# A fourth extra chunk place for the first model's experts, with the fetch order changed to suit it

## The chip, the cores and the metric

The kernel runs on one core of a Trainium2 chip. The metric is device time in microseconds (us) of one execution. The kernel before takes 2479.06 us, the median of three runs (2478.96 to 2481.82).

## The reference, cut to what matters

Two small models run one after the other on 256 tokens of width 1024, two layers each, all in float32. Every layer has a mixer (attention in the first model; retention, an RWKV recurrence and a short convolution in the second) and then a layer of 32 experts of which every token uses two. The change lies in the expert layers of the first model:

```python
def hierarchical_moe(xn, w_group, w_router, w_gate, w_up, w_down):
    ...
    group_p = jax.nn.softmax((xt @ w_group).astype(jnp.float32), axis=-1)
    group_w, group_id = lax.top_k(group_p, 1)
    ...
    top_logits, local_id = lax.top_k(in_group, TOP_K_IN_GROUP)      # 2 of 4 experts in the group
    ...
    def expert_block(args):
        xb, e = args
        h = jax.nn.silu(xb @ w_gate[e]) * (xb @ w_up[e])            # 1024 -> 256
        return h @ w_down[e]                                        # 256 -> 1024
    ...
    y = jax.ops.segment_sum(contrib, tok_sorted, num_segments=T)
```

## The kernel before, in words

**Weights.** All weights come from HBM in chunks of 128 x 4096 float32 (2 MB), each by one DMA that SP (SyncE) issues in program order on one hardware queue. They land in `ring`, six places of that size. A chunk's arrival counts on `w_loaded`, its last use by TensorE on `w_used`; SP waits for `w_used` before it lets a new chunk overwrite a place.

**The expert layer** is the function `moe`. It is called four times: for both layers of the first model (experts 256 wide, "shared" in the code; here stage 1 and stage 2) and for both layers of the second (experts 512 wide). Experts go by quads, four at a time, eight quads in all. In the first model a quad has six chunks: 0 to 3 hold gate and up weights, 4 and 5 the down weights. I write (2,3) for chunk 3 of quad 2, and count quads from 0. A quad's work is an *item*: up to 32 tokens of each of its four experts. If an expert of the quad has more tokens, the quad is done again with the next 32, so the number of items depends on the data; every engine loops over a count that VectorE works out.

**One item on TensorE**, in its own order: gate and up products (L2031, 64 records), `combine` of the item before (L1990: the weighted sum of its outputs back to the tokens, 16 records), `gather` of the next item's tokens (L1982, 32 records), two pairs of transposes (L2042, L2046), and the down products (L2056, 32 records, half of them for chunk 4 and half for chunk 5). The first item has no item before it, so its `combine` multiplies tables that GpSimd has set to zero (L2124, L2125). The gather of item 1 waits for a one-hot table from VectorE (L2140), and that for the routing tables (`tables_ready`, L2216).

**Fetching in the first model** (L1921 to L1939). The ring alone would hold one quad. So three *extra places* in `arena` take chunks 0, 1 and 2 of the next quad, while the current one is in use. GpSimd waits until all three have landed (L2130), then copies each into the ring as soon as the last item of the current quad has used its place (L2131 to L2133). SP's order for quad q is: (q,3) straight into the ring after the last item of quad q-1 has used its fourth gate/up chunk; then (q+1,0), (q+1,1), (q+1,2) into the extra places, each after GpSimd has copied out what was there; then (q,4) and (q,5) after their places were used. Before the tables are ready SP can't know which item is a quad's last, so it waits for them ahead of that loop. After the loop it fetches the next layer's first six chunks as places come free.

**Before the stage** the six chunks of quad 0 and one extra chunk are fetched during the attention's output projection (L838); the other extra ones are issued at the stage's start (L1921).

**The second model's experts** have twelve chunks a quad. They use the same `moe`, with another fetch loop that has no copies.

## Time and profile before

| what | us |
|---|---|
| median of three runs | 2479.06 |
| the profiled execution | 2471.02 |
| its span, from first to last instruction | 2469.2 |
| TensorE busy | 2018.6 (82%) |
| VectorE, ScalarE, GpSimd busy | 634.9, 377.5, 205.5 |
| bytes read from HBM | 776.75 MB, 315 GB/s over the span |
| mean granted TensorE clock | 0.923 of full |

The page cuts the span into 40 slices of 61.7 us. Stage 1 (157 to 380 us) lies in slices 3 to 6, stage 2 (520 to 760 us) in slices 9 to 12, and the second model's expert layers in slices 20 to 26 and 34 to 40. In all of them the DMA engines are nearly always busy, at some 430 GB/s, and TensorE is partly idle. Outside them TensorE is busy and the DMA engines partly idle. In the listings of instructions "idle before <- releaser" says how long the engine stood idle before a group, and what ended the wait. Several instructions of one line in a row are merged into one line of a listing, with a count. Matmuls are counted twice (float32 takes two passes), so a line of 8 in the program shows as 16.

### The profile page before, as it was taken

The numbers are of one execution on the slowest core, as the hardware profiler recorded it, in microseconds if no ns is written. First come the engines' busy times: TensorE is split into PE (matmuls) and PEld (weight loads), VectorE is DVE, ScalarE is ACT, GpSimd is POOL, SyncE is SP. The second block draws the span as 40 slices with busy tenths as digits, with TensorE's granted clock in tenths as the row PEclk, the third lists the DMA queues.
The fourth block names the chain that finished last, engine by engine and source line by source line (L and its number), as shares of the span: only waits on it lengthen the run. The fifth ranks groups of instructions, "written<-read, shape, count | busy, mean of one in ns | idle before, by whom it ended". The sixth has DMA issues, their size and how long they took to land. (4 is left out here: it accounts for less than half of the span.)

```text
span 2469.2 us, 33765 instructions
## 1 busy us (share of the span) xinstructions
PE 2018.6 (82%) x14228; PEld 1282.1 (52%) x14229; DVE 634.9 (26%) x1483; ACT 377.5 (15%) x817; POOL 205.5 (8%) x140
## 2 busy tenths in 40 slices
PE   8997779998778999999866666599999998666665
PEld 6573336574334888888322222148888873222222
DVE  4651114531113245463100000032551121000001
ACT  2520001511002121101100000021221020000001
POOL 0213330214330000000000000000000000000000
PEclk9998889999889999999988888899999998888888
DMA  8569998449997241497999999963302389999997
GB/s 341 232 281 431 430 430 365 163 180 421 431 430 298 103 160 47 200 397 301 402 428 429 429 429 428 427 273 113 141 34 103 136 341 428 429 429 428 428 428 302
DMA packets 55842, 779.34 MB, mean 316 GB/s; under 512 B 6841, under 2 KB 7097, under 8 KB 8121
## 3 DMA queue, kind: packets, MB, share of 16 engines
q1 hardware_dynamic: 55736, 777.82, 75.7%
q8 instruction: 80, 1.31, 0.2%
q14 instruction: 26, 0.20, 0.0%
HBM read 776.75 MB, written 1.05 MB: 315 GB/s over the span
## 5 line engine op out<-in xcount | busy, mean ns | idle before, releaser
L2031 PE MATMUL bank<-ring,xnT 128*32 128x512 f32 x3136 | 446.8, 712 | 234.1 <-DMA ring<-in_w_exp 233.8
L2031 PEld LDWEIGHTS bank<-ring,xnT 128*32 128x32 f32 x3136 | 101.4, 121 | 573.4 <-issue 292.3
L2056 PE MATMUL bank<-ring,arena 128*32 128x512 f32 x1440 | 201.2, 696 | 148.1 <-DMA ring<-in_w_exp 126.7
L1023 PE MATMUL bank<-xnT,ring 128*128 128x256 f32 x960 | 210.7, 379 | 0.0
L1023 PEld LDWEIGHTS bank<-xnT,ring 128*128 128x128 f32 x960 | 181.6, 190 | 28.4 <-issue 4.5
L2056 PEld LDWEIGHTS bank<-ring,arena 128*32 128x32 f32 x1440 | 48.8, 120 | 273.4 <-issue 155.4
L2229 DVE TENSOR_TENSOR arena<-bank,arena 128x256 f32<-128x256 f32 (+1 forms) x33 | 18.3, 554 | 609.5 <-PE bank L2031 520.5
L1709 PE MATMUL bank<-xnT,ring 128*128 128x256 f32 x768 | 173.6, 379 | 0.0
L2133 POOL COPY ring<-arena 128x4096 f32<-128x4096 f32 x42 | 150.5, 3620 | 261.4 <-DMA arena<-in_w_exp 232.7
L1709 PEld LDWEIGHTS bank<-xnT,ring 128*128 128x128 f32 x768 | 146.1, 190 | 22.1 <-issue 2.5
L1990 PE MATMUL bank<-arena,xnT 128*128 128x256 f32 x592 | 142.0, 394 | 0.0
L1990 PEld LDWEIGHTS bank<-arena,xnT 128*128 128x128 f32 x592 | 112.7, 196 | 53.8 <-issue 35.1
L1982 PE MATMUL bank<-arena 128*128 128x128 f32 x1056 | 123.7, 275 | 0.2 <-DVE arena L2140 0.2
L1982 PEld LDWEIGHTS bank<-arena 128*128 128x128 f32 x1056 | 122.7, 192 | 2.3 <-DVE arena L2140 0.6
L251 DVE SCALAR_TENSOR_TENSOR arena<-arena 128x1024 f32<-128x1024 f32 x96 | 112.6, 1223 | 29.9 <-DMA arena<-in_w_ada 29.4
L2240 DVE COPY xnT<-bank 128x512 f32<-128x512 f32 x33 | 22.8, 692 | 320.3 <-PE bank L2056 320.3
L1716 PE MATMUL bank<-arena,ring 128*128 128x256 f32 x384 | 90.7, 379 | 0.0
L1017 PE MATMUL bank<-ring,xnT 128*128 128x512 f32 x192 | 84.4, 602 | 6.4 <-ACT xnT L375 6.4
L1716 PEld LDWEIGHTS bank<-arena,ring 128*128 128x128 f32 x384 | 73.0, 190 | 9.9
L2104 ACT ACTIVATE arena<-bank 128x256 f32<-128x256 f32 (+1 forms) x33 | 16.1, 487 | 398.7 <-PE bank L2031 398.7
L2085 ACT ACTIVATE xnT<-bank,mod,gains 128x128 f32<-128x128 f32 x64 | 24.1, 456 | 325.8 <-PE bank L1982 325.8
L1198 POOL TENSOR_TENSOR arena<-arena,pc 128x1024 f32<-128x1024 f32 x2 | 3.9, 1952 | 792.8 <-DVE arena L1300 792.8
(439 smaller groups left out, 2081.9 us busy)
## 6 DMA issues: line engine op xcount, KB each, us to landing
ring<-in_w_exp SPq DMA_DIRECT2D x238, 2048.0 KB, 25.6
arena<-in_w_exp SPq DMA_DIRECT2D x50, 2048.0 KB, 16.9
arena<-in_w_ada SPq DMA_DIRECT2D x24, 2048.0 KB, 11.3
ring<-in_w_in SPq DMA_DIRECT2D x20, 2048.0 KB, 23.2
ring<-in_w_merge SPq DMA_DIRECT2D x18, 2048.0 KB, 8.0
ring<-in_w_o SPq DMA_DIRECT2D x8, 2048.0 KB, 11.8
ring<-in_w_conv SPq DMA_DIRECT2D x6, 2048.0 KB, 8.0
ring<-in_w_rest SPq DMA_DIRECT2D x2, 1696.0 KB, 14.1
```

The source lines that it names most:

```text
L251: last = nc.vector.scalar_tensor_tensor(w, w, 1.0, c, ALU.mult, ALU.mult, accum_out=mod_sums[:, l, 4 * ch + j:4 * ch + j + 1])
L1017: last = nc.tensor.matmul(o[:, 0:MW], xnT[:, k, P * (not first):P * (not first) + P], w[:, k, :], start=k == 0, stop=k == KT - 1)
L1023: last = nc.tensor.matmul(o[:, T * j:T * j + T], w[:, k, col:col + P], xnT[:, k, :], start=k == 0, stop=k == KT - 1)
L1709: last = nc.tensor.matmul(bank[m % 8][:, 0:T], w[:, k, P * (d % 4):P * (d % 4) + P], xnT[:, k, :], start=k == 0, stop=k == KT - 1)
L1716: last = nc.tensor.matmul(bank[m % 8][:, T:2 * T], w[:, k, P * d:P * d + P], ys[i][:, k, :], start=k == 0, stop=k == MT - 1)
L1982: last = nc.tensor.matmul(gather_banks[d // 4][:, P * (d % 4):P * (d % 4) + P], xtok[:, t, P * d:P * d + P], onehot[:, t, :], start=t == 0 ...
L1990: last = nc.tensor.matmul(bank[d // 2][:, T * (d % 2):T * (d % 2) + T], Yw[:, P * d:P * d + P], gwT, start=False, stop=ready is not None, ...
L2031: last = nc.tensor.matmul(o[rows(e), :], Xw[:, k, rows(e)], w[:, at:at + MW], start=k == 0, stop=k == KT - 1)
L2056: last = nc.tensor.matmul(o[rows(e), :], hidT[:, j, rows(e)], w[:, at:at + MW], start=j == 0, stop=j == ft - 1)
L2085: last = nc.scalar.activation(Xw[:, d, :], at_d, ACT.Identity, scale=gain[:, d:d + 1], bias=shift[:, d:d + 1])
L2133: nc.gpsimd.tensor_copy(ring[:, place(r0 + n), :], extra[spots[n]]).then_inc(w_loaded(slot(n)), 16)
L2240: nc.vector.tensor_copy(Yw[:, 0:MW], y0_bank[:, :]).then_inc(y0_taken, 1)
```

## The change

- `EXTRA1` goes from 3 to 4: all four gate/up chunks of the next quad have an extra place. GpSimd copies four chunks a quad in place of three, and waits for four landings first.
- SP's order for quad q becomes (q,4), then (q+1,0) to (q+1,3), then (q,5). The first fetch of a quad now waits for the last item's first *down* chunk (`w_used`, `n0 + EXTRA1 + 1`).
- The extra places become consecutive. The third one covers ground in `arena` where the stage's small tables and the vector `c_all` lay. The tables move to `small`. `c_all` moves to the part of the constants that only the second model uses. That part (1032 of 2429 columns) is therefore not loaded at the start; it is loaded in stage 2, behind the next layer's vectors, and the first model's final norm waits for it.
- The first item of every expert layer, in both models, no longer runs `combine`. GpSimd no longer sets those two tables to zero.

```diff
-EXTRA1, EXTRA2 = 3, 4
+EXTRA1, EXTRA2 = 4, 4
...
-        c_all = ar(15744, D)
+        CST2 = CONST["ret_in"][0]
+        c_all = cst[:, CST2:CST2 + D]
...
-                    sp.dma_start(cst[:], dram["consts"]).then_inc(cst_loaded, 16)
+                    sp.dma_start(cst[:, 0:CST2], dram["consts"][:, 0:CST2]).then_inc(cst_loaded, 16)
...
-            at = 13824
+            at = 0 if shared else SMALL2
             extras = EXTRA1 if shared else EXTRA2
-            spots = (0, 1, 3) if shared else (0, 1, 2, 3)
...
                     if after:
                         vectors_early(sp, *after, 1 - turn[0])
+                    if shared and after[0] == 2:
+                        sp.dma_start(cst[:, CST2:], dram["consts"][:, CST2:]).then_inc(cst2_loaded, 16)
...
                             for n in range(EXTRA1 if q + 1 < NQ else 0):
                                 sp.wait_ge(w_loaded(slot(n)), 16 * ((r0 + n) // RING + 1) + 16 * q)
-                                sp.dma_start(extra[spots[n]], feed(q + 1, n)).then_inc(extra_in, 16)
+                                sp.dma_start(extra[n], feed(q + 1, n)).then_inc(extra_in, 16)
...
                         pe.wait_ge(y0_taken, it + 1)
-                        pe.wait_ge(gwT_ready, it + 1)
-                        combine()
+                        if not first_item:
+                            pe.wait_ge(gwT_ready, it + 1)
+                            combine()
...
-                    nc.gpsimd.memset(gate_tab[:, NE * TT:(NQ + 1) * QUAD * TT], 0.0)
-                    nc.gpsimd.memset(gwT, 0.0)
-                    nc.gpsimd.memset(Yw, 0.0).then_inc(gwT_ready, 1)
+                    nc.gpsimd.memset(gate_tab[:, NE * TT:(NQ + 1) * QUAD * TT], 0.0).then_inc(gwT_ready, 1)
...
                         dve.wait_ge(gw_turned, it + 1)
+                        dve.wait_ge(gwT_ready, it + 1)
                         nc.vector.tensor_copy(gwT, y0_bank[:, 0:T]).then_inc(gwT_ready, 1)
```

SP's queue at the start of stage 1, before. L1921 fills the extra places, L225 loads the next layer's vectors, L1916 is a fetch into the ring and L1936 one into an extra place:

```order
L1921 DMA arena<-in_w_exp1 128x4096 x2
L225 DMA vec<-in_vec1 128x27 [waits e1_tables]
L225 DMA row<-in_row1 1x8
L225 DMA small<-in_small1 128x2880
L1931 TENSOR_LOAD offs
L1931 ISA x2
L1932 REGISTER_ALU
L1916 DMA ring<-in_w_exp1 128x4096 [waits w_used0]
L1936 DMA arena<-in_w_exp1 128x4096 [waits w_loaded0_0]
L1936 DMA arena<-in_w_exp1 128x4096 [waits w_loaded0_1]
L1936 DMA arena<-in_w_exp1 128x4096 [waits w_loaded0_2]
L1938 REGISTER_ALU
```

And now (the same places have the lines L1922, L1917 and L1939):

```order
L1922 DMA arena<-in_w_exp1 128x4096 x3
L225 DMA vec<-in_vec1 128x27 [waits e1_tables]
L225 DMA row<-in_row1 1x8
L225 DMA small<-in_small1 128x2880
L1934 TENSOR_LOAD offs
L1934 ISA x2
L1935 REGISTER_ALU
L1917 DMA ring<-in_w_exp1 128x4096 [waits w_used0]
L1939 DMA arena<-in_w_exp1 128x4096 [waits w_loaded0_0]
L1939 DMA arena<-in_w_exp1 128x4096 [waits w_loaded0_1]
L1939 DMA arena<-in_w_exp1 128x4096 [waits w_loaded0_2]
L1939 DMA arena<-in_w_exp1 128x4096 [waits w_loaded0_3]
```

Three chunks stand ahead of the tables in place of two. The ring fetch behind them was (1,3) and is now (1,4), and its wait on `w_used` is for one chunk more of the item. Everything behind it in the queue stands behind that wait.

TensorE in the first item of stage 1, before, from its last gate/up chunk to the transposes:

```order
L2031 MATMUL bank<-ring,xnT 32x512 [waits w_loaded0_3]
L2031 MATMUL bank<-ring,xnT 32x512 x7
L1990 MATMUL bank<-arena,xnT 128x256 [waits e1_gwT,e1_y0taken]
L1990 MATMUL bank<-arena,xnT 128x256 x7
L1982 MATMUL bank<-arena 128x128 [waits e1_onehot]
L1982 MATMUL bank<-arena 128x128 x15
L2042 MATMUL bank<-cst,arena 128x128 [waits e1_hid]
L2042 MATMUL bank<-cst,arena 128x128
```

And now:

```order
L2034 MATMUL bank<-ring,xnT 32x512 [waits w_loaded0_3]
L2034 MATMUL bank<-ring,xnT 32x512 x7
L1985 MATMUL bank<-arena 128x128 [waits e1_onehot,e1_y0taken]
L1985 MATMUL bank<-arena 128x128 x15
L2046 MATMUL bank<-cst,arena 128x128 [waits e1_hid]
L2046 MATMUL bank<-cst,arena 128x128
```

The eight matmuls of `combine` are gone, and the gather's wait for the one-hot table stands right behind the gate/up products.

## Rows read from the trace of the kernel before

**Rows 1.** The page: DMA share by slice, and the costliest groups of the expert stages.

```profile
DMA  8569998449997241497999999963302389999997
...
L2031 PE MATMUL bank<-ring,xnT 128*32 128x512 f32 x3136 | 446.8, 712 | 234.1 <-DMA ring<-in_w_exp 233.8
...
L2133 POOL COPY ring<-arena 128x4096 f32<-128x4096 f32 x42 | 150.5, 3620 | 261.4 <-DMA arena<-in_w_exp 232.7
```

**Rows 2.** Stage 2, stretches: PE, PEld, DVE, ACT, POOL busy; clock, DMA share, GB/s.

```profile
530.00:540.00 10.00, 10.00 (x80) 5.46 (x73) 4.85 (x27) 0.38 (x1) 0.00 (x0) 1.00 0.70 275
540.00:550.00 10.00, 8.79 (x83) 4.86 (x85) 2.91 (x8) 2.10 (x6) 0.00 (x0) 1.00 0.00 0
550.00:560.00 10.00, 10.00 (x80) 5.81 (x73) 0.42 (x1) 0.38 (x1) 9.71 (x3) 1.00 0.39 129
```

**Rows 3.** TensorE in stage 1, in time: start, length, what, idle before.

```profile
177.27 3.84 PE L1982 MATMUL bank<-arena 128*128 128x128 f32 x32 [0.16 <-DVE arena L2140]
...
182.70 3.64 PE L2056 MATMUL bank<-ring,arena 128*32 128x512 f32 x32 [1.16 <-ACT arena L2109]
...
205.11 3.51 PE L2056 MATMUL bank<-ring,arena 128*32 128x512 f32 x16 [4.02 <-DMA ring<-in_w_exp]
...
351.16 3.64 PE L2056 MATMUL bank<-ring,arena 128*32 128x512 f32 x16 [7.72 <-DMA ring<-in_w_exp]
355.96 1.92 PE L2056 MATMUL bank<-ring,arena 128*32 128x512 f32 x16 [1.16 <-DMA ring<-in_w_exp]
357.92 7.07 PE L2031 MATMUL bank<-ring,xnT 128*32 128x512 f32 x64
364.93 3.72 PE L1990 MATMUL bank<-arena,xnT 128*128 128x256 f32 x16
...
369.61 3.64 PE L2056 MATMUL bank<-ring,arena 128*32 128x512 f32 x32 [0.53 <-DVE arena L2234]
```

**Rows 4.** TensorE in stage 2, in time.

```profile
539.18 3.73 PE L1982 MATMUL bank<-arena 128*128 128x128 f32 x32
...
544.51 3.64 PE L2056 MATMUL bank<-ring,arena 128*32 128x512 f32 x32 [1.16 <-ACT arena L2109]
...
564.09 3.64 PE L2056 MATMUL bank<-ring,arena 128*32 128x512 f32 x32 [1.16 <-ACT arena L2109]
...
733.75 3.64 PE L2056 MATMUL bank<-ring,arena 128*32 128x512 f32 x16 [1.16 <-DMA ring<-in_w_exp]
```

**Rows 5.** VectorE in time: the one-hot table, in stage 1 and 2.

```profile
174.37 2.84 DVE L2140 TENSOR_TENSOR arena<-cst,arena 128x256 f32<-128x256 f32 x1 [2.07 <-issue]
...
536.31 0.43 DVE L2140 TENSOR_TENSOR arena<-cst,arena 128x256 f32<-128x256 f32 x1 [1.78 <-issue]
```

**Rows 6.** SP in time: the first ring fetch of stage 1 and 2.

```profile
174.31 0.33 SPq L1916 DMA_DIRECT2D ring<-in_w_exp  x1
...
555.33 0.33 SPq L1916 DMA_DIRECT2D ring<-in_w_exp  x1
```

**Rows 7.** One microsecond stretches in stage 1, columns as in group 2.

```profile
171.00:172.00 1.00, 1.00 (x14) 0.27 (x10) 0.97 (x12) 0.00 (x0) 0.00 (x0) 1.00 0.24 98
172.00:173.00 1.00, 1.00 (x16) 0.25 (x8) 0.23 (x3) 0.00 (x0) 0.00 (x0) 1.00 0.00 0
```

**Rows 8.** GpSimd in time: first and last group of copies in stage 1.

```profile
173.34 10.88 POOL L2133 COPY ring<-arena 128x4096 f32<-128x4096 f32 x3 [15.00 <-DMA arena<-in_w_exp]
...
346.33 10.69 POOL L2133 COPY ring<-arena 128x4096 f32<-128x4096 f32 x3 [18.52 <-DMA arena<-in_w_exp]
```

**Rows 9.** VectorE in time, at the program's start.

```profile
9.53 0.17 DVE L296 CAST arena<-arena 128x4 f32<-128x4 int32 x1 [9.40 <-DMA arena<-in_positions]
...
17.73 3.26 DVE L367 SCALAR_TENSOR_TENSOR xnT<-hT,vec,arena 128x256 f32<-128x256 f32 x8 [0.31 <-PEq L278]
```

**Rows 10.** TensorE in the second model's first expert layer, in time.

```profile
1196.56 4.71 PE L1990 MATMUL bank<-arena,xnT 128*128 128x256 f32 x16
...
1223.99 1.92 PE L2031 MATMUL bank<-ring,xnT 128*32 128x512 f32 x16 [1.43 <-DMA ring<-in_w_exp]
```

More of the change, by code:

```diff
@@ L75, in constants @@
         put(f"freq{half}", np.tile(freq.astype(np.float32)[None, :], (P, 1)))
+    put("pair", p[:, None] % HD == np.arange(HEADS // 2)[None, :])
+    put("iota", np.tile(np.arange(1.0, 33.0)[None, :], (P, 1)))
     lg = np.log1p(-np.exp2(-5.0 - np.arange(RH, dtype=np.float32))).astype(np.float32)
@@ L87, in constants @@
     put("unit", at == to)
-    put("pair", p[:, None] % HD == np.arange(HEADS // 2)[None, :])
-    put("iota", np.tile(np.arange(1.0, 33.0)[None, :], (P, 1)))
     put("inner", np.tile((np.arange(T) % CH != 0)[None, :], (P, 1)))
@@ L259, in build @@
         c_loaded = sem("c_loaded")
+        cst2_loaded = sem("cst2_loaded")
         def sines(act, c_ready):
@@ L1878, in ar @@
                 size = int(np.prod(shape))
-                v = (arena[0:n, o:o + size] if shared else small[0:n, o - at + SMALL2:o - at + SMALL2 + size])
+                v = small[0:n, o:o + size]
                 if len(shape) == 2:
@@ L1920, in _ @@
                             continue
-                        sp.dma_start(extra[spots[e]], feed(1, e) if shared else feed(0, kept + e)).then_inc(extra_in, 16)
+                        sp.dma_start(extra[e], feed(1, e) if shared else feed(0, kept + e)).then_inc(extra_in, 16)
                     for n in range(RING, kept):
@@ L2010, in here @@
                                 pe.wait_ge(extra_in, 16 * extras)
-                                return extra[spots[n - kept]]
+                                return extra[n - kept]
                             if first_item and held:
@@ L2132, in _ @@
                                 pool.wait_ge(w_used(), last_item + (n0 + n + 1))
-                                nc.gpsimd.tensor_copy(ring[:, place(r0 + n), :], extra[spots[n]]).then_inc(w_loaded(slot(n)), 16)
+                                nc.gpsimd.tensor_copy(ring[:, place(r0 + n), :], extra[n]).then_inc(w_loaded(slot(n)), 16)
                 @block.vector
@@ L2280, in _ @@
                     norm_sums(pe, norms, bank[0])
+                    pe.wait_ge(cst2_loaded, 16)
                 @block.vector
@@ L2310, in build @@
                 head_rms_out(l, ada, extra_in)
-                moe("e1", lambda q, n: dram["w_exp1"][l, 6 * q + n], MOE1, F1, extra_in, (2,), NG1, gains[:, 1, :], None, None, (1, 1) if l + 1 < L else (2, 0))
+                moe("e1", lambda q, n: dram["w_exp1"][l, 6 * q + n], MOE1, F1, extra_in, (3,), NG1, gains[:, 1, :], None, None, (1, 1) if l + 1 < L else (2, 0))
                 next_layer(MOE1)
```

## The prediction

> **What bounds the kernel now.** I read the page first. The line of DMA shares shows 9 in the slices of the expert stages, and TensorE's costliest group, the gate/up products, stands idle 234.1 us of which 233.8 us end with a weight's landing [rows 1]. So in these stages the transfers decide, not the matmuls. Then I read stage 1 in order of time: the down products of quad 1 wait until 205.11 us for chunk 4, those of quad 6 until 351.16 us [rows 3]. Between them lie five quads of six chunks, so a chunk takes (351.16 - 205.11) / 30 = 4.868 us, and a quad 29.2 us. TensorE needs less: one item is 19.6 us where nothing waits (544.51 to 564.09 us) [rows 4]. Third, I looked for stretches without transfers inside the stages, because only there can another place help. In stage 1 the hole is short, about 2.5 us near 172 us [rows 7]. In stage 2 it is long: the DMA share is 0.70, 0.00 and 0.39 in three stretches of 10 us [rows 2]. There quad 0 has two items, and SP may not fetch (1,3) before the second has used its gate/up chunks, at 555.33 us [rows 6].
>
> **What ends a stage.** This decides the sum, so it comes before the parts. The last landing that TensorE waits for in stage 1 is (6,5): its products start at 355.96 us. From there on nothing waits for a transfer: item 7 runs 357.92, 364.93, 369.61 us, and the wait before the last is 0.53 us for VectorE [rows 3]. So the stage's end is the landing of (6,5) plus a fixed chain on TensorE. Now count the chunks that the queue carries from the first ring fetch through (6,5). Before: (1,3), (1,4), (1,5), the 30 chunks of quads 2 to 6, and (7,0) to (7,2), which is 36. After: (1,4), (1,5), the same 30, and (7,0) to (7,3), which is 36 again. The fourth place takes (1,3) out at the front and puts (7,3) in at the back. Nothing is saved on the way. What matters is when the queue starts again, and how long the chain behind (6,5) is.
>
> **The later restart.** Seen from TensorE, the stream of 36 chunks began at 355.96 - 36 x 4.868 = 180.7 us in stage 1 and at 733.75 - 175.2 = 558.5 us in stage 2 [rows 3, 4]. In stage 2 the queue was empty when (1,3) was issued, so issue to effective start costs 558.5 - 555.33 = 3.2 us [rows 6].
> - Stage 2 after. (1,4) waits for the first down chunk of item 1. Its products began at 564.09 us and half of them are done 1.8 us later, at 565.9 us [rows 4]. The removed `combine` of item 0 gives some of it back, but not its whole 3.7 us: the gather that then follows needs the one-hot table, which ends at 536.31 + 0.43 = 536.74 us, while the gather now starts at 539.18 us [rows 4, 5]. So 2.4 us. (1,4) is issued at about 563.6 us, the stream starts at 566.8 us: +8.3 us.
> - Stage 1 after. The same with one item: half the down products at 182.70 + 1.8 = 184.5 us [rows 3]. The gather can start when the table is there. It took 2.84 us beside GpSimd's copies, which began at 173.34 us, against 0.43 us in stage 2 where GpSimd waits [rows 5, 8]. After, GpSimd waits for a fourth landing, some 4.9 us later, so I take 0.43 us: table at 174.8 us, gather 2.4 us earlier than its 177.27 us. (1,4) is issued at 182.2 us and the stream starts at 185.4 us: +4.7 us. By then the queue is empty: one chunk more ends at about 171.3 + 4.9 = 176.2 us, and the next layer's small table (1.5 MB, 3.4 us at the rate of a chunk) near 180 us. If the one-hot table took 2.84 us after all, it would be +7.1 us.
>
> The Trainium skill, "DMA: Bandwidth & Descriptors", in its part on the chain of events of a DMA, gives a fixed cost of about 2.0 us beside the bytes. The 3.2 us that I read are more than that; with 2.0 us both restarts would be 1.2 us earlier and the sum below 2.4 us smaller. I stay with the row.
>
> **The longer chain behind (6,5).** GpSimd began its last three copies 9.6 us before (6,5) was there and took 10.7 us [rows 8]. In the new order (7,3) is the last before (6,5), so the copies begin one chunk time, about 4.8 us, before it, and there are four: 4 x 3.6 = 14.4 us [rows 1]. The last ends 9.6 us after the landing and its products 1.8 us later: 11.4 us. Before, the gate/up products ended at 364.99 us, 9.0 us after [rows 3]. Each stage: +2.4 us. TensorE now gets these chunks at the pace of the copies, half of the time busy. After 7.72 us of waiting 16 records took 3.64 us, the lower clock level of 1.2 GHz, and the next 16 after 1.16 us of waiting 1.92 us, at 2.4 GHz [rows 3]. If the last gate/up chunk and the `combine` behind it run low, they cost 1.8 and 1.0 us more (4.71 us against 3.72 us for a `combine` behind such a stretch) [rows 3, 10]. Bounds 0 and 2.8 us a stage, also if all is at the high level; I take 0.5 us each, since copies at 3.6 us leave shorter waits than those before 351.16 us.
>
> The Trainium skill speaks against the change here: "TensorE: Matmul & The Clock Gate", section "HAM oscillation — how this bites in real kernels", says that bursts of matmuls shorter than the transfer wait between them all start on the slow clock. By that rule the sum would be 4.6 us higher (2 x 2.8 instead of 2 x 0.5). The trace agrees at 351.16 us and not at 355.96 us.
>
> **The start.** 1032 of 2429 columns of the constants, 0.53 MB, leave the queue ahead of the positions. VectorE waits for these until 9.53 us and its chain then runs to the norm at 17.73 us [rows 9]. At 430 GB/s that is 1.2 us earlier, and everything behind it: -1.2 us (bounds -1.2 and 0, if TensorE's or ScalarE's chain is next).
>
> **Edits that I cost at nothing.** The other half of the constants, 1.2 us of transfer, falls into the hole of stage 2 [rows 2]; without the hole it would be +1.2 us. 14 more copies (50.7 us) fit into GpSimd's waits, 18.5 us a quad [rows 8]. The zeroed tables were off the path. In the second model the first `combine` (4.71 us) goes too, but the queue behind is never empty and TensorE soon waits for a chunk again, at 1223.99 us [rows 10]: 0, at best -0.5 us. VectorE's new wait is for the copy of the item before, long done. The moved tables are read by the same instructions.
>
> **The sum**, against the profiled execution of 2471.0 us: -1.2 + (4.7 + 2.4 + 0.5) + (8.3 + 2.4 + 0.5) = +17.6 us, so 2488.6 us. Behind each stage TensorE has no wait for a weight until the mixer, so the delay is passed on. The three timed runs had a median 8.0 us above the profiled one; carried over, 2496.7 us. I say 2496 us.
>
> **The rivals.**
> - *A hole in every quad* (10%). (q+1,4) waits for the first down chunk of quad q, and all extra chunks stand behind it. The copies for quad q end 19.6 us before the landing of (q,5), gate/up 17.8 us; from there to the down products it is 8.8 us (555.3 to 564.09 us) [rows 4, 6], and 1.8 us for half of them: issue 7.2 us before, seen 8.1 us later at the earliest, which is 4.0 us earlier than the stream needs it. If slow clocks and slower tables take 5 us instead of the 2.8 us above, 1 us is lost in each of five quads of both stages: +10 us, 2507 us. For it speaks the 3.64 us row, against it that the margin is 4 us.
> - *The last landing sets the end* (8%). If (7,5) and the next layer's chunks behind it decided, each stage would get its chunk back: -1.2 + (4.7 - 4.9) + (8.3 - 4.9) = +2.0 us, 2481 us. Against it stand the 0.53 us wait and the missing DMA waits behind 355.96 us [rows 3].
> - *The other side: one chunk less in the bound stretch* (6%). If, besides, the restart were not later, because the queue lasts until the first down chunk is used, the time would be -1.2 - 2 x 4.9 = -11 us, 2468 us. It decides whether the queue is still full at 182 and at 564 us. For stage 1 only 2 us are missing; in stage 2 the queue is empty more than 20 us before.
> - The forecast has 74%, its own range 2490 to 2502 us; 2% is for what I don't see.
>
> **How the numbers follow.** What this measurement can tell from no change is about 0.2%, 5 us. Slower: 74 + 10 + 2 = 86%. Same: 7%. Faster: 7%. The range of 2483 to 2508 us holds the forecast with the bounds of its terms and the lower part of the holes; it leaves out the last two rivals, 14%.
>
> **What would show it.** In the trace after: the first ring fetch of the stages at about 181 and 561 us (182.2 and 563.6 us less the 1.2 us of the start, the second plus the 7.6 us of stage 1, so near 570 us); DMA share 1.00 from there until item 7; the last quad's gate/up products in four bursts 3.6 us apart; the norm behind stage 1 at some 6.4 us later than now. It is wrong if TensorE waits for (7,5), if the first ring fetch is issued while the queue is still busy, or if a stretch inside quads 2 to 6 shows a DMA share well below 1.

## The result, and the profile after

The changed kernel takes 2497.64 us, the median of seven runs (2487.99 to 2504.74). The kernel before, run beside it on the same chip, took 2479.06 us (seven runs, 2473.29 to 2481.82). The ratio is 1.0078, with a 95% interval of 1.006 to 1.0096: slower by 0.8%. The forecast was 2496 us.

The profiled execution after took 2499.79 us with a span of 2497.9 us and a mean granted clock of 0.916, against 2471.02, 2469.2 and 0.923 before. The page after, as in [rows 1] (DMA share by slice, then line, engine, operation, count | busy us, mean ns of one | idle before, and what ended it):

```profile
DMA  8569998448997331397899999963312379999997
...
L2034 PE MATMUL bank<-ring,xnT 128*32 128x512 f32 x3136 | 460.2, 727 | 247.3 <-DMA ring<-in_w_exp 236.5
...
L2135 POOL COPY ring<-arena 128x4096 f32<-128x4096 f32 x56 | 201.5, 3641 | 246.0 <-DMA arena<-in_w_exp 215.4
```

The DMA line hardly shows the change: of the slices of stages 1 and 2 only the tenth (562 to 624 us of the span after) goes from 9 to 8, since the hole of stage 2 now reaches into it. The gate/up products wait 13.2 us longer in all, and only 2.7 us more of it for DMA. The other waits go from 0.3 to 10.8 us, 10.5 us of them for GpSimd's copies. These are now 56 and not 42, at the same length.

The page shows where, the rows in time show how much. The same stretches of stage 2 after (columns as in [rows 2]):

```profile
560.00:570.00 10.00, 8.84 (x64) 7.46 (x68) 2.68 (x7) 1.90 (x6) 9.20 (x3) 1.00 0.00 0
570.00:580.00 10.00, 9.98 (x91) 3.19 (x84) 1.12 (x2) 0.97 (x2) 0.00 (x0) 1.00 0.82 323
```

In stage 1 the hole is short, but it is there before the restart too:

```profile
178.00:180.00 2.00, 1.38 (x16) 0.59 (x20) 1.82 (x3) 0.00 (x0) 2.00 (x1) 1.00 0.08 33
```

SP after, the first ring fetch of stages 1 and 2 and the fetches behind it (as in [rows 6]):

```profile
180.59 0.33 SPq L1917 DMA_DIRECT2D ring<-in_w_exp  x1
180.97 3.21 SPq L1939 DMA_DIRECT2D arena<-in_w_exp  x2
...
570.75 0.33 SPq L1917 DMA_DIRECT2D ring<-in_w_exp  x1
571.12 2.41 SPq L1939 DMA_DIRECT2D arena<-in_w_exp  x4
```

The prediction had these at about 181 and near 570 us. TensorE at the start of stage 1 after (start, length, what, idle before and what ended it; compare the first two rows of [rows 3]):

```profile
173.21 3.81 PE L1985 MATMUL bank<-arena 128*128 128x128 f32 x32 [1.50 <-DVE arena L2142]
...
178.62 3.64 PE L2060 MATMUL bank<-ring,arena 128*32 128x512 f32 x32 [1.16 <-ACT arena L2113]
```

178.62 us and half of 3.64 us is 180.44 us; the fetch is issued at 180.59 us. So it does wait for the first half of the down products. And TensorE at the end of stage 1 after, the last five rows of [rows 3]:

```profile
350.68 1.92 PE L2060 MATMUL bank<-ring,arena 128*32 128x512 f32 x16 [1.16 <-ACT arena L2113]
359.38 3.64 PE L2060 MATMUL bank<-ring,arena 128*32 128x512 f32 x16 [6.78 <-DMA ring<-in_w_exp]
362.80 5.89 PE L2034 MATMUL bank<-ring,xnT 128*32 128x512 f32 x48
368.95 1.92 PE L2034 MATMUL bank<-ring,xnT 128*32 128x512 f32 x16 [0.26 <-POOL ring L2135]
370.81 3.72 PE L1993 MATMUL bank<-arena,xnT 128*128 128x256 f32 x16
375.48 3.64 PE L2060 MATMUL bank<-ring,arena 128*32 128x512 f32 x32 [0.52 <-DVE arena L2237]
```

The landing of (6,5) is the last one waited for, at 359.38 us; there is no DMA wait behind it, so (7,5) doesn't set the end. The last gate/up chunk waits for GpSimd and is done at 370.87 us, 11.5 us after the landing; 11.4 us was the sum. GpSimd after, the last quad but one and the last (as in [rows 8]):

```profile
325.46 14.42 POOL L2135 COPY ring<-arena 128x4096 f32<-128x4096 f32 x4 [14.72 <-DMA arena<-in_w_exp]
354.67 14.23 POOL L2135 COPY ring<-arena 128x4096 f32<-128x4096 f32 x4 [14.78 <-DMA arena<-in_w_exp]
```

**The ledger.** I take as a stage's start its first transposes of the tokens (L1964 before, L1967 after) and as its end the first matmul of the norm behind it (L361, L363). All in us, from the two profiled executions:

| part of the program | before | after | difference |
|---|---|---|---|
| start to stage 1 | 157.14 | 155.39 | -1.75 |
| stage 1, to the landing of (6,5) | 198.82 | 203.99 | +5.17 |
| stage 1, landing to the end | 20.78 | 23.23 | +2.45 |
| between the stages | 143.69 | 141.70 | -1.99 |
| stage 2, to the landing of (6,5) | 213.32 | 224.60 | +11.28 |
| stage 2, landing to the end | 22.50 | 23.19 | +0.69 |
| behind stage 2 | 1712.95 | 1725.80 | +12.85 |
| span | 2469.2 | 2497.9 | +28.7 |

The start and the two stages make +17.8 us, close to the difference of the medians (18.6 us). The two other rows need not be the change. Behind stage 2 the first experiment below speaks for that: it has the program of before there, word for word, and takes 1726.2 us (2498.3 - 772.08).

### The profile page after: what moved, and what is told of

Its sections match the earlier page's. It is cut to its first block and busy times, and to the rows that moved or that the text cites. A ratio compares the mean times of both kernels' runs of the same rounds, so it can differ in the third digit from the quotient of the medians.

```text
span 2497.9 us, 33692 instructions
## 1 busy us (share of the span) xinstructions
PE 2022.7 (81%) x14164; PEld 1283.6 (51%) x14165; DVE 639.7 (26%) x1483; ACT 378.0 (15%) x817; POOL 252.0 (10%) x146
## 5 line engine op out<-in xcount | busy, mean ns | idle before, releaser
L2034 PE MATMUL bank<-ring,xnT 128*32 128x512 f32 x3136 | 460.2, 727 | 247.3 <-DMA ring<-in_w_exp 236.5
L2060 PE MATMUL bank<-ring,arena 128*32 128x512 f32 x1440 | 192.9, 672 | 159.5 <-DMA ring<-in_w_exp 125.3
L2135 POOL COPY ring<-arena 128x4096 f32<-128x4096 f32 x56 | 201.5, 3641 | 246.0 <-DMA arena<-in_w_exp 215.4
L1985 PEld LDWEIGHTS bank<-arena 128*128 128x128 f32 x1056 | 128.3, 199 | 9.5 <-issue 7.7
L1985 PE MATMUL bank<-arena 128*128 128x128 f32 x1056 | 129.8, 283 | 3.0 <-DVE arena L2142 3.0
L1993 PE MATMUL bank<-arena,xnT 128*128 128x256 f32 x528 | 126.4, 393 | 0.0
L1993 PEld LDWEIGHTS bank<-arena,xnT 128*128 128x128 f32 x528 | 100.3, 195 | 49.5 <-issue 31.6
L2115 ACT COPY xnT<-bank 128x512 f32<-128x512 f32 x33 | 19.3, 585 | 320.8 <-PE bank L2060 320.8
## 6 DMA issues: line engine op xcount, KB each, us to landing
ring<-in_w_exp SPq DMA_DIRECT2D x224, 2048.0 KB, 25.6
ring<-in_w_rest SPq DMA_DIRECT2D x2, 1696.0 KB, 10.8
```

The costliest lines, as they stand in the source:

```text
L1985: last = nc.tensor.matmul(gather_banks[d // 4][:, P * (d % 4):P * (d % 4) + P], xtok[:, t, P * d:P * d + P], onehot[:, t, :], start=t == 0 ...
L1993: last = nc.tensor.matmul(bank[d // 2][:, T * (d % 2):T * (d % 2) + T], Yw[:, P * d:P * d + P], gwT, start=False, stop=ready is not None, ...
L2034: last = nc.tensor.matmul(o[rows(e), :], Xw[:, k, rows(e)], w[:, at:at + MW], start=k == 0, stop=k == KT - 1)
L2060: last = nc.tensor.matmul(o[rows(e), :], hidT[:, j, rows(e)], w[:, at:at + MW], start=j == 0, stop=j == ft - 1)
L2115: nc.scalar.copy(Yw[:, MW:D], y1_bank[:, :]).then_inc(y1_taken, 1)
L2135: nc.gpsimd.tensor_copy(ring[:, place(r0 + n), :], extra[n]).then_inc(w_loaded(slot(n)), 16)
```

## The experiments

One table for all, from each one's profiled execution. "Fetch" is the first fetch behind the tables, (6,5) its landing, both counted from the stage's start, as is the length. The ratio is against runs of the kernel before, taken beside it on the same chip; e1 to e4 ran on one chip, e5 to e8 on another.

| kernel | ratio (95%) | stage 1: fetch, (6,5), length | stage 2: fetch, (6,5), length |
|---|---|---|---|
| before | | 17.17, 198.82, 219.60 | 34.90, 213.32, 235.82 |
| after | 1.0078 (1.006 to 1.0096) | 25.20, 203.99, 227.22 | 46.44, 224.60, 247.79 |
| e1 late restart | 1.0091 (1.0066 to 1.0116) | 27.62, 206.53, 227.29 | 46.68, 225.20, 247.48 |
| e2 zeros back | 1.012 (1.0082 to 1.0158) | 26.05, 204.71, 228.00 | 48.66, 226.85, 250.04 |
| e3 small edits alone | 1.0003 (0.9978 to 1.0028) | 17.16, 199.20, 219.96 | 34.26, 212.66, 235.21 |
| e4 extras first | 1.0025 (1.0005 to 1.0045) | 24.80, 203.50, 225.69 | 34.25, 212.41, 233.17 |
| e5 split places | 0.9959 (0.9943 to 0.9974) | 18.40, 194.64, 216.94 | 32.84, 206.11, 228.74 |
| e6 three places first | 1.0048 (1.0027 to 1.0068) | 19.83, -, 225.39 | 34.58, -, 239.03 |
| e7 one more copy | one run, 2525.86 us | 25.06, 209.14, 239.11 | 46.26, 229.74, 259.60 |
| e8 two more copies | one run, 2553.53 us | 25.21, 219.80, 253.31 | 46.19, 240.16, 273.43 |

**e1, late restart: the kernel before, and only the first ring fetch of the stage waits for the first down chunk.**

```diff
-                            sp.wait_ge(w_used(), last_item + (n0 + EXTRA1 + 1))
+                            sp.wait_ge(w_used(), last_item + (n0 + EXTRA1 + (2 if q == 1 else 1)))
                             fetch(q, EXTRA1)
```

> The kernel before with three extra places; only the first ring fetch of each stage of the first model waits, as in the changed kernel, for the first down chunk of quad 0's last item, not for its fourth gate/up chunk. No fourth place. My theory (the stage ends at the landing of (6,5) plus a fixed chain, so a later restart of the queue is paid in full): first ring fetch near 184.6 us in stage 1 (174.3 before) and 565.9 us plus the delay of stage 1 in stage 2 (555.3 before); the down products of (6,5) 7 us later in stage 1 (184.6 + 3.2 against 180.7 effective) and 10.5 us later in stage 2; no change of the chain behind (364.99 - 355.96 = 9.0 us to the end of gate/up). Sum +17.5 us, ratio 1.007. Rival 'the last landing sets the end, or other slack hides it': the norm behind each stage moves by under 2 us, ratio 1.000 to 1.002.

Measured: 2496.15 against 2473.18 us; the expected 1.007 is inside the interval. SP and TensorE of e1, first fetch of stages 1 and 2, and the last landing of stage 1:

```profile
183.23 0.33 SPq L1916 DMA_DIRECT2D ring<-in_w_exp  x1
...
571.28 0.33 SPq L1916 DMA_DIRECT2D ring<-in_w_exp  x1
```

```profile
362.14 1.92 PE L2056 MATMUL bank<-ring,arena 128*32 128x512 f32 x16 [1.15 <-DMA ring<-in_w_exp]
364.10 7.07 PE L2031 MATMUL bank<-ring,xnT 128*32 128x512 f32 x64
```

One number changed in a wait gives a loss as large as that of the whole change: the stages are 7.7 and 11.7 us longer. In stage 2 about 1.1 us of this is the clock: the first transposes took 3.58 us, where they took 1.94 us before. The chain behind the landing is here the old, short one (9.0 us, no wait for a copy). So the two terms are separate: e1 has the restart later by 7.7 us and no longer chain; the change has 5.2 us of restart and 2.45 us of chain. The 2.4 us between the two first fetches are in the main the `combine` that the change takes away and e1 keeps.

**e2, zeros back: the kernel after, with the first `combine` and its zeroed tables again.**

```diff
-                        if not first_item:
-                            pe.wait_ge(gwT_ready, it + 1)
-                            combine()
+                        pe.wait_ge(gwT_ready, it + 1)
+                        combine()
```

> The changed kernel with the first item's combine and the zeroed tables put back in all four expert layers. Theory: the gather of item 1 starts behind combine again, so in the first model's stages the first ring fetch comes about 2 us later than in the changed kernel (180.6 us and 570.8 us there), the landing of (6,5) with it; nothing in the second model, where the queue never runs dry: +4 to +4.5 us in all, ratio to before 1.0095. Rival 'all of combine is on the path, in all four layers': +3.7 us four times, +15 us, ratio 1.0135. Rival 'hidden': 0.

Measured: 2505.42 against 2473.18 us. The first fetch of stage 2 comes 2.2 us later than in the changed kernel, for 2.4 us in the sum, and the stage ends 2.25 us later. In stage 1 it is only 0.85 us. There this execution's first transposes ran at the higher clock (1.94 us for 3.35 us), and the gate/up products began 1.07 us earlier after the stage's start (8.18 us for 9.25 us). Without that it would be 1.9 us: less than in stage 2, because in the changed kernel the gather stands 1.50 us waiting for the one-hot table where `combine` was. The ratio is 0.0042 above that of the changed kernel, 10 us for the 4.1 us that I explain; the intervals overlap, so that isn't told apart from noise. The ratio alone doesn't exclude the rival "all of `combine`, in all four layers" (1.0135) either. The traces do: the stages show 1.9 and 2.2 us and not 3.7 us each, and behind stage 2 e2 takes 1727.5 us for 1725.8 us, not 7.4 us more. What is shown is that removing `combine` helps, and that without it the restart would come later still.

**e3, small edits alone: the kernel before, three places, its order of fetches, with the constants split and the first `combine` gone.** The diff is that of the change without `EXTRA1`, the places and the tables.

> The kernel before with only the two small edits: the constants' second half is loaded in stage 2, and the first item runs no combine. Three extra places and the old fetch order. Theory: start -1.2 to -1.8 us; stage 1: first ring fetch not moved relative to the stage's start (it waits for gate/up, which combine follows), so 0; stage 2: quad 0 has two items and the second comes 2.4 us earlier, so the first ring fetch, the landing of (6,5) and the stage's end 2.4 us earlier relative to the stage's start. Sum -4 us, ratio 0.9985. Rival 'nothing': ratio 1.000 and the same times in the trace. Rival 'all of combine counts': -1.5 - 4 x 3.7 = -16 us, ratio 0.9934.

Measured: 2471.98 against 2473.18 us, inconclusive by time: both the expected 0.9985 and no change at all lie inside the interval. In the trace stage 1 begins 1.65 us earlier, so the split of the constants does what it should. But the first fetch of stage 1 stands where it stood, 17.16 us after the start. With three places its wait is for the fourth gate/up chunk, ahead of `combine`. Stage 2 gets 0.6 us, where 2.4 us was expected. Counted from the stage's first gate/up products, the first fetch is indeed 2.3 us earlier (24.45 us for 26.71 us). But these products begin 1.6 us later after the stage's start than before (9.81 us for 8.19 us), because the gather ahead of them took 5.46 us, and 3.84 us in the kernel before:

```profile
520.27 5.46 PE L1986 MATMUL bank<-arena 128*128 128x128 f32 x32 [0.22 <-DVE arena L2143]
```

The granted clock was 0.50 from 522 to 524 us. This gather takes 5.46 or 5.47 us in all eight kernels of this study that have the small edits, and 3.84 us in the two without (before and e1). Why is not shown. VectorE and GpSimd of e3 show the other thing that I had used:

```profile
172.73 2.99 DVE L2143 TENSOR_TENSOR arena<-cst,arena 128x256 f32<-128x256 f32 x1 [2.08 <-issue]
...
171.85 10.88 POOL L2136 COPY ring<-arena 128x4096 f32<-128x4096 f32 x3 [16.29 <-PE bank L2035]
```

Beside GpSimd's copies the one-hot table takes 2.99 us. In the changed kernel, where these copies begin at 176.49 us, the same instruction runs before them:

```profile
172.64 0.43 DVE L2142 TENSOR_TENSOR arena<-cst,arena 128x256 f32<-128x256 f32 x1 [2.08 <-issue]
```

The forecast took 0.43 us for it, by that reason.

**e4, extras first: the kernel after, but SP's order for a quad is the four extra chunks, then (q,4) and (q,5).**

```diff
-                            sp.wait_ge(w_used(), last_item + (n0 + EXTRA1 + 1))
-                            fetch(q, EXTRA1)
                             for n in range(EXTRA1 if q + 1 < NQ else 0):
...
-                            for n in range(EXTRA1 + 1, RING):
+                            for n in range(EXTRA1, RING):
```

> The changed kernel with SP's order turned: in each quad first the four extra fetches, then (q,4), then (q,5). Theory: the queue restarts when GpSimd has copied the first chunk out (started 176.5 us in stage 1, 555.0 us in stage 2 of the changed kernel, plus 3.6 us), so first fetch behind the tables at 180.1 and 558.6 us against 180.6 and 570.8 us: -0.5 and -12 us. The copies begin two chunk times before (6,5) instead of one, so the chain behind it is bound by TensorE's 7 us of gate/up: -0.9 us a stage. Sum -14 us against the changed kernel, ratio to before 1.002. Rival 'the later restart isn't what costs; the copies or the slow clock are': the time stays within 4 us of the changed kernel, ratio 1.006 to 1.009.

Measured: 2480.68 against 2473.18 us, in the profile 2479.29 us. The restart no longer waits for the down chunk, and the first fetch of stage 2 is back at 34.25 us. SP of e4:

```profile
177.79 4.07 SPq L1937 DMA_DIRECT2D arena<-in_w_exp  x2
...
554.62 3.87 SPq L1937 DMA_DIRECT2D arena<-in_w_exp  x2
```

The ratio of 1.0025 is what was expected. Stage 2 is then 2.65 us shorter than before, where the changed kernel's was 12 us longer: the order, not the fourth place, costs stage 2. Nor does the place gain anything there: e3 has three places, e4 has four, both carry 36 chunks from a first fetch at 34.26 and 34.25 us, and (6,5) lands at 212.66 and 212.41 us. Stage 1 is still 6.1 us longer. There the first fetch waits for GpSimd's first copy, and GpSimd waits until all four extra chunks have landed.

**e5, split places: e4 with one semaphore for each extra place, and the fourth extra chunk behind (q,5).**

```diff
-                            for n in range(EXTRA1 if q + 1 < NQ else 0):
+                            for n in range(EXTRA1 - 1 if q + 1 < NQ else 0):
...
-                            for n in range(EXTRA1 + 1, RING):
+                            for n in range(EXTRA1, RING):
                                 sp.wait_ge(w_used(), last_item + (n0 + n + 1))
                                 fetch(q, n)
+                            if q + 1 < NQ:
+                                take_extra(EXTRA1 - 1)
...
-                            pool.wait_ge(extra_in, 16 * extras * q)
                             for n in range(EXTRA1):
+                                pool.wait_ge(extra_in[n], 16 * q)
```

(`take_extra(n)` is the old wait and fetch, counting on `extra_in[n]`.)

> The changed kernel with a semaphore for each extra place, so that GpSimd copies a chunk as soon as it has landed and its ring place is free, and with SP's order per quad (q+1,0), (q+1,1), (q+1,2), (q,4), (q,5), (q+1,3): no fetch waits for a down chunk before the queue has restarted, and (7,3) comes behind (6,5). Theory: through (6,5) there are now 35 chunks behind the restart, not 36, with one more fetched before it. Stage 1 seen from its start: the queue hardly runs dry, (6,5) some 3.5 us earlier than in the kernel before (198.8 us after the stage's start there), the chain behind it 10.3 us to the end of gate/up instead of 9.0: -2 us. Stage 2: restart at the first copy, -3.8 us, and one chunk less, -4.9 us, so (6,5) 8.7 us earlier (213.3 us after the stage's start before): -8 us. With the start's -1.5 us: -12 us against the kernel before, ratio 0.995. Rival 'the copies by GpSimd are the burden of the fourth place': slower than before still, 1.003 or more. Rival 'the restart decides alone, the count of chunks doesn't': -1.5 - 3.8 = -5 us, ratio 0.998.

Measured: 2464.26 us (11 runs) against 2475.3 us (18 runs): faster than the kernel before by 0.4%, and than the changed one by 1.2% (0.9959 / 1.0078). SP, GpSimd and TensorE of e5:

```profile
172.81 4.07 SPq L1937 DMA_DIRECT2D arena<-in_w_exp  x2
```

```profile
208.16 3.60 POOL L2137 COPY ring<-arena 128x4096 f32<-128x4096 f32 x1 [11.02 <-DMA arena<-in_w_exp]
213.01 3.60 POOL L2137 COPY ring<-arena 128x4096 f32<-128x4096 f32 x1 [1.25 <-DMA arena<-in_w_exp]
217.86 3.60 POOL L2137 COPY ring<-arena 128x4096 f32<-128x4096 f32 x1 [1.25 <-DMA arena<-in_w_exp]
```

```profile
344.25 3.64 PE L2062 MATMUL bank<-ring,arena 128*32 128x512 f32 x16 [5.66 <-DMA ring<-in_w_exp]
349.05 1.92 PE L2062 MATMUL bank<-ring,arena 128*32 128x512 f32 x16 [1.16 <-DMA ring<-in_w_exp]
351.01 5.36 PE L2036 MATMUL bank<-ring,xnT 128*32 128x512 f32 x48
357.70 1.92 PE L2036 MATMUL bank<-ring,xnT 128*32 128x512 f32 x16 [1.33 <-POOL ring L2137]
```

The copies follow the landings one by one. The first fetch is early again in both stages. In stage 1 that is the work of the semaphores alone, since the fourth chunk's new position changes nothing ahead of it: the copies begin 14.8 us after the stage's start, for 21.2 us in e4. And (7,3) now stands behind (6,5), so up to this landing the queue carries 35 chunks, not 36: here the fourth place does save a chunk. The landing comes 4.2 and 7.2 us earlier than in the kernel before. Counting as the prediction did for stage 2: 32.84 + 3.2 + 35 x 4.868 = 206.4 us, measured 206.11 us. In stage 1 the same count gives 192.0 us for a measured 194.64 us; there the queue wasn't empty when the first fetch was issued (DMA share 0.99 from 171 to 173 us), so the stream doesn't start at the fetch. The two edits of e5 weren't run apart.

**e6, three places first: three extra places, the small edits, the extra chunks first and then (q,3), (q,4), (q,5).** The diff is e4's on top of e3.

> Three extra places as before, with the two small edits of the first experiment on them (constants split, no first combine), and SP's order turned: first the three extra fetches of a quad, then (q,3), (q,4), (q,5). Theory: the queue restarts at the end of GpSimd's first copy; in stage 2 that is 1.8 + 3.6 us after the start of item 1's gate/up instead of 7.1 us, so 1.7 us earlier than with the same edits and the old order (34.3 us after the stage's start), (6,5) as much earlier; stage 1 as before, since the table's transfer covers the restart. Against the kernel before: start -1.5, stage 1 0, stage 2 -2.4 - 1.7: -5.5 us, ratio 0.998. What it is short of the version with the fourth place and its own semaphores is what the place itself is worth: one chunk time a stage where the queue stood idle, near 5 us in stage 2 and 2 us in stage 1.

Measured: 2485.76 against 2475.3 us, a miss: I expected a gain. TensorE of e6 at the end of stage 1:

```profile
344.97 3.64 PE L2033 MATMUL bank<-ring,xnT 128*32 128x512 f32 x16 [7.67 <-DMA ring<-in_w_exp]
348.54 4.52 PE L1992 MATMUL bank<-arena,xnT 128*128 128x256 f32 x16
352.89 3.73 PE L1984 MATMUL bank<-arena 128*128 128x128 f32 x32
...
358.23 3.64 PE L2059 MATMUL bank<-ring,arena 128*32 128x512 f32 x32 [1.16 <-ACT arena L2112]
361.89 7.07 PE L2033 MATMUL bank<-ring,xnT 128*32 128x512 f32 x64
```

I had counted chunks up to (6,5). In this order the last landing that TensorE waits for is another one: (6,3), for the last gate/up products of item 6, at 344.97 us. Behind it stand `combine`, the gather, the transposes and both halves of the down products, until 361.87 us. The down products run in one piece with no DMA wait, so (6,5) was there by 358.23 us; two chunks behind (6,3) it would land at about 354.7 us, an estimate. The count of chunks says when a landing comes, but the chain that follows counts as much: 35.7 us lie between the wait for (6,3) and the norm at 380.70 us, where 20.8 us followed (6,5) before. So (6,3), 189.66 us after the stage's start, ends the stage at 225.39 us.

**e7 and e8, one and two more copies: the kernel after, where GpSimd copies one extra place onto itself once or twice in each quad, ahead of the last copy.** That delays the last gate/up chunk, and with it the down products for which (q+1,4) waits. It asks how large the margin of the first rival is.

```diff
                                 nc.gpsimd.tensor_copy(ring[:, place(r0 + n), :], extra[n]).then_inc(w_loaded(slot(n)), 16)
+                                for i in range(1 if n == 2 else 0):
+                                    nc.gpsimd.tensor_copy(extra[3], extra[3]).then_inc(slowed, 1)
+                                    pool.wait_ge(slowed, 1 * (q - 1) + i + 1)
```

> The changed kernel with one more copy of 3.6 us on GpSimd in each quad (the fourth extra place onto itself, between the copies of chunks 2 and 3). Theory: the margin of (q+1,4) is about 3.5 to 4 us, so no hole opens in quads 2 to 6: the landings of (6,5) unmoved relative to the stage's start (204.0 and 224.6 us after it in the changed kernel), and the chain behind each 3.6 us longer (15.1 us from the landing to the end of gate/up, 11.5 us now): +3.6 us a stage. Rival 'GpSimd's copies are covered': 0. Rival 'the margin is used up already': some us for every quad, (6,5) later by 10 us or more.

> The same with two such copies, 7.2 us in each quad. Theory: now the margin is gone. A quad in two finds its (q+1,4) issued 3.3 us too late, which alternates with one that isn't: 29.2 us a quad becomes 30.5 to 31 us, (6,5) some 6 to 7 us later in each stage, the chain 7.2 us longer: +14 us a stage. Rival 'the margin is much more than 4 us': (6,5) unmoved, +7.2 us a stage.

Measured: the stages are 11.9 and 11.8 us longer than in the changed kernel with one more copy, 26.1 and 25.6 us with two. Both forecasts (+3.6 and +14 us a stage) were too small, and e7's was wrong in kind: it said that no hole opens with one copy. TensorE of e7 at the end of stage 1:

```profile
363.77 1.92 PE L2061 MATMUL bank<-ring,arena 128*32 128x512 f32 x16 [1.28 <-DMA ring<-in_w_exp]
365.73 3.64 PE L2035 MATMUL bank<-ring,xnT 128*32 128x512 f32 x32
...
377.32 3.64 PE L2035 MATMUL bank<-ring,xnT 128*32 128x512 f32 x16 [5.33 <-POOL ring L2136]
```

The chain from the landing to the end of the gate/up products (380.96 us) is 17.2 us, against 11.5 us: +5.7 us from one copy of 3.8 us (186.84 to 190.65 us in the first quad, its wait included). Most of the rest is the clock. TensorE stands 5.33 us before its last chunk, and then runs it at 3.64 us instead of 1.92 us, at a granted clock of 0.50. With two copies, 8.99 us of waiting, the same 3.64 us, and +9.3 us in all. Then (6,5) itself is late, by 5.1 and 15.8 us. The loss comes in pairs of quads: in e7 the wait for a second down chunk ends at 241.68, 302.73 and 363.77 us, every 61.05 us, where two quads need 58.33 us (301.05 to 359.38 us in the changed kernel). In e8 it is 64.8 us. So a pair loses 2.7 us when the chain is 5.7 us longer, and 6.5 us when it is 9.3 us longer; both leave a margin of about 3 us. Two stretches of e8 show the hole (columns as in [rows 2]):

```profile
208.00:211.00 3.00, 1.84 (x21) 1.63 (x21) 1.60 (x6) 1.13 (x4) 3.00 (x1) 1.00 0.95 404
211.00:214.00 3.00, 3.00 (x28) 0.84 (x32) 0.38 (x1) 0.10 (x1) 3.00 (x2) 1.00 0.29 60
```

The changed kernel has none: over quads 1 to 6 of stage 1 its DMA engines are never idle.

```profile
190.00:360.00 170.00, 114.77 (x828) 58.89 (x832) 22.66 (x52) 14.30 (x41) 78.53 (x23) 0.88 1.01 431
```

## Why the prediction was right, step by step

- **The count of 36 chunks and the last landing.** Right. After, the landing of (6,5) minus 36 x 4.868 us gives an effective start of 184.1 us in stage 1, 3.5 us behind the fetch, and 573.7 us in stage 2, 2.9 us behind it. The forecast used 3.2 us for both. The fixed cost of about 2.0 us that the Trainium skill gives ("DMA: Bandwidth & Descriptors", the chain of events of a DMA) is less than either; its fit is for transfers issued from GpSimd, and these are SP's.
- **The later restart.** Right: +4.7 us forecast and +5.17 us measured in stage 1. But there the down chunk isn't the only thing that holds the queue: e4, which waits for GpSimd's first copy instead, restarts 24.80 us after the stage's start, for 25.20 us, and the prediction didn't see this second bound. In stage 2 +8.3 us was forecast and +11.28 us measured to the landing, of which about 3.05 us are clock. Before, the gate/up products of that stage began 8.19 us after its start, and after the change 11.24 us, although no instruction of TensorE in between was edited. These are the rows of before and of after:

```profile
520.43 1.94 PE L1964 MATMUL bank<-cst,hT 128*128 128x128 f32 x16 [0.71 <-PEq L833]
524.85 3.84 PE L1982 MATMUL bank<-arena 128*128 128x128 f32 x32
528.62 7.07 PE L2031 MATMUL bank<-ring,xnT 128*32 128x512 f32 x64
```

```profile
524.31 3.60 PE L1967 MATMUL bank<-cst,hT 128*128 128x128 f32 x16 [0.71 <-PEq L835]
530.15 5.47 PE L1985 MATMUL bank<-arena 128*128 128x128 f32 x32 [0.34 <-DVE arena L2142]
535.55 7.08 PE L2034 MATMUL bank<-ring,xnT 128*32 128x512 f32 x64
```

  The same 16 transposes take 1.94 us at 2.4 GHz (granted clock 1.00) and 3.60 us at 1.2 GHz (0.50), and the gather behind them 3.84 and 5.47 us. Without that, 8.2 us. The transposes ran low in seven of the ten profiled executions, in no order by what was edited. The gather is another matter: its 1.6 us come with the small edits (see e3). The sum had nothing for them, and why they arise stays open.
- **The longer chain.** +2.4 us forecast, +2.45 us in stage 1, +0.69 us in stage 2. Here a size was wrong. The working took "9.0 us after" from stage 1 for both stages. In stage 2 the chain of before ran its down products at the low clock (3.64 us, [rows 4]) and its gate/up products in 7.36 us, so it ended 10.8 us after the landing, not 9.0. The row stood in the groups, and I should have used it. After, both are about 11.45 us.
- **The clock term.** 0.5 us a stage, for the last chunk at the low clock. It was 0: the wait before the last chunk was 0.26 and 0.43 us, and the products ran in 1.92 us. Nor did the four bursts 3.6 us apart show that the prediction had named as a sign: TensorE came to these products only at 362.80 us, ran three chunks of them in one piece (48 records in 5.89 us), and waited for the fourth copy alone. The rule from the Trainium skill, "TensorE: Matmul & The Clock Gate" (bursts shorter than their waits all run slow), had been priced at 2.8 us a stage. The case that it speaks of didn't arise here, since these waits were shorter than the bursts; the wait of 1.16 us before 355.96 us in the kernel before was no such case either, so what didn't fit was the prediction's use of the rule. The traces agree with the rule where the last wait is 5.33 and 8.99 us (e7, e8): the burst behind it takes 3.64 us.
- **The start.** -1.2 us forecast, -1.43 us measured at the norm (16.30 us, for 17.73 us in [rows 9]) and -1.75 us at the stage's start. VectorE after:

```profile
8.10 0.17 DVE L298 CAST arena<-arena 128x4 f32<-128x4 int32 x1 [7.97 <-DMA arena<-in_positions]
...
16.30 2.07 DVE L369 SCALAR_TENSOR_TENSOR xnT<-hT,vec,arena 128x256 f32<-128x256 f32 x5 [0.31 <-PEq L280]
```

- **The sum.** Stage 1 was forecast 7.6 us longer and is 7.62 us longer; stage 2 11.2 and 11.97 us. Part of this exactness is luck. In stage 2 the restart gave 8.2 us as forecast, but the chain only 0.7 us instead of 2.4 us and the clock term nothing instead of 0.5 us; the slower start of the stage, for which the sum had no term, more than made up for both with 3.05 us.
- **The rivals.** The hole in every quad didn't come. (6,4) was issued when the first down chunk of quad 5 had been used, at 323.5 us, and the products that wait for (5,5) begin at 330.22 us. That is 6.7 us where the working had 7.2, and e7 and e8 put the margin at about 3 us, not 4. The mechanism is real: e7 and e8 call it up. "The last landing sets the end" fell with the missing DMA waits; "one chunk less" fell because the queue was idle at both restarts (share 0.00 from 560 to 570 us, 0.08 from 178 to 180 us).

What the profiled execution shows beyond the sum (-2.0 us between the stages, +12.85 us behind) goes with the granted clock: 0.98 before and 0.99 after between the stages, 0.93 and 0.91 behind stage 2. Behind stage 2 the ten profiled executions of this study lie between 1713.0 us (the kernel before) and 1727.5 us (e2), with no order by what was changed. That the before profile is the lowest of all explains why the spans differ by 28.7 us and the medians by 18.6 us.

## What to carry to other kernels

A prefetch place buys nothing while the same number of transfers stands ahead of the last landing that is waited for: count them from the moment the queue starts again, and add the chain of work behind *that* landing, which in a new order may be another one (e6). The place paid here when its transfer moved behind the last landing that matters, with the copies following their landings one by one, each on its own semaphore (e5, both edits together). And a wait moved to a later event in an in-order queue costs its full length where the queue is empty, as at the start of each stage here (e1).

## What was not expected of the hardware

- One VectorE operation on two inputs in SBUF, 128x256 float32, took 0.43 us alone and 2.84 and 2.99 us ([rows 5], e3) beside a GpSimd copy of a chunk. Its length is not its own: in both it ended 3.87 us after that copy had begun (173.34 and 171.85 us), just behind the end of a copy of 3.6 us. In the changed kernel the next such operation took 3.83 us, begun at 183.81 us amid the copies. The sum rested on this difference.
- The span moves with the clock by about as much as with this change: seven runs of the changed kernel lie between 2485.9 us (mean granted clock 0.925) and 2502.7 us (0.910). A comparison of two profiles is worth little before the stretches that differ only in clock are taken out.
- A delay of 3.8 us in a copy that TensorE waits for lengthened the chain by 5.7 us, since the burst behind the 5.33 us of waiting ran at the low clock: 3.64 us for 1.92 us.
- The gather at the start of stage 2 took 5.47 us in every kernel with the small edits and 3.84 us in the two without, and no row shows the reason.
